# Two attention stages on one core: another order of VectorE's work inside each turn

## The reference, cut to what matters

```python
# sliding window, first block
scores = jnp.where(valid, scores + bias, NEG_INF)
probs = jax.nn.softmax(jnp.concatenate([scores, sink], axis=-1), axis=-1)[..., :-1]
out = jnp.einsum('bnhgqk,bnkhd->bnqhgd', probs, vb)
...
# chunk band and causal, second block
p = jax.nn.softmax(sc, axis=-1)
return jnp.einsum('bhqk,bhkd->bhqd', p, v)
```

## Time and profile before

| what | us |
|---|---|
| median of 3 executions | 1940.71 |
| lowest of them | 1938.64 |
| the profiled execution, its own time | 1938.64 |
| its span in the trace | 1936.6 |
| TensorE matmuls busy | 1904.5 (98% of the span) |
| TensorE weight loads busy | 1577.2 (81%) |
| VectorE busy | 968.0 (50%) |
| ScalarE busy | 778.3 (40%) |
| GpSimd busy | 92.8 (5%) |

### The profile page before, as it was taken

The page is one execution under the profiler, slowest core; times in us unless marked ns, Lnnn a source line. Parts: engine busy times, 40 slices in busy tenths (PEclk is TensorE's granted clock), DMA queues, the critical chain, the costliest instruction groups (busy, mean ns, idle before and its releaser), DMA issues.

```text
span 1936.6 us, 23640 instructions
## 1 busy us (share of the span) xinstructions
PE 1904.5 (98%) x9297; PEld 1577.2 (81%) x9297; DVE 968.0 (50%) x2069; ACT 778.3 (40%) x1482; POOL 92.8 (5%) x165
## 2 busy tenths in 40 slices
PE   8999999999999999999999999999999999999998
PEld 6888888868888888887888888888888888888887
DVE  5788764546676666665321244433343433333234
ACT  5566333347777777776211132312030312212022
POOL 4111001100000000000000000000000000000000
PEclk9999999999999999999999999999999999999999
DMA  5410124322232212222321141212020211112002
GB/s 169 115 34 28 55 87 152 102 67 66 61 77 72 74 52 64 74 61 59 95 54 44 55 159 48 66 44 66 22 76 23 75 33 55 55 33 66 22 22 87
DMA packets 132479, 129.29 MB, mean 67 GB/s; under 512 B 7233, under 2 KB 112265, under 8 KB 132370
## 3 DMA queue, kind: packets, MB, share of 16 engines
q1 hardware_dynamic: 126482, 115.18, 19.7%
q0 software_dynamic: 5888, 12.62, 2.9%
HBM read 105.70 MB, written 15.79 MB: 63 GB/s over the span
## 4 chain that ended last, share of the span: by engine, by line
PE 89%; DVE 6%; ACT 3%; issue 2%; DMA 0%; POOL 0%; DVEq 0%; POOLq 0%; SPq 0%; ACTq 0%
PE b L86 85%; PE b L89 4%; DVE Wf L108 1%; DVE Wr L97 1%; ACT Wf L94 1%; DVE Xr L97 1%; ACT Wf L93 1%; DVE Wf L97 1%; ACT Wr L93 1%; DVE ring L97 1%; ACT Xr L93 0%; DVE Yf L105 0%; DVE Wf L101 0%; DVE Yr L105 0%; ACT ring L93 0%
## 5 line engine op out<-in xcount | busy, mean ns | idle before, releaser
L86 PE MATMUL b<-Yr,ring 128*128 128x512 f32 x1920 | 507.9, 400 | 1.1 <-DVE Xr L97 1.1
L86 PE MATMUL b<-Xr,ring 128*128 128x512 f32 x1872 | 452.7, 393 | 3.3 <-DVE Xr L97 1.5
L86 PEld LDWEIGHTS b<-Xr,ring 128*128 128x128 f32 x1872 | 345.6, 189 | 70.9 <-issue 4.2
L86 PEld LDWEIGHTS b<-Yr,ring 128*128 128x128 f32 x1920 | 340.1, 189 | 56.0 <-DVE Xr L97 1.5
L86 PE MATMUL b<-Xr,Yr 128*128 128x512 f32 x1104 | 254.0, 390 | 0.0
L86 PEld LDWEIGHTS b<-Xr,Yr 128*128 128x128 f32 x1104 | 206.8, 188 | 42.8
L86 PE MATMUL b<-Yr 128*128 128x512 f32 (+2 forms) x1040 | 236.1, 375 | 0.0
L86 PEld LDWEIGHTS b<-Yr 128*128 128x128 f32 x1040 | 190.7, 188 | 38.1
L97 DVE TENSOR_TENSOR Wf<-Wf,b 128x512 f32<-128x512 f32 x144 | 92.6, 684 | 237.7 <-PE b L86 237.7
L93 ACT ACTIVATE Wf<-b 128x512 f32<-128x512 f32 (+3 forms) x215 | 106.2, 494 | 229.1 <-PE b L86 225.5
L94 ACT ACTIVATE Wf<-Wf,st 128x640 f32<-128x640 f32 (+3 forms) x192 | 125.2, 652 | 162.1 <-DVE st L112 58.8
(11 more groups left out here) (123 smaller groups left out, 1612.6 us busy)
## 6 DMA issues: line engine op xcount, KB each, us to landing
stage<-in_w_in_dram SPq DMA_DIRECT2D x58, 512.0 KB, 4.0
stage<-in_w_up_dram SPq DMA_DIRECT2D x32, 512.0 KB, 4.0
stage<-in_w_down_dram SPq DMA_DIRECT2D x32, 512.0 KB, 3.5
stage<-in_w_out_dram SPq DMA_DIRECT2D x16, 512.0 KB, 3.5
Xr<-Xr POOLq DMA_DIRECT2D x32, 256.0 KB, 3.4
Yf<-in_x_dram SPq DMA_DIRECT2D x8, 512.0 KB, 6.4
Wf<-in_x_dram SPq DMA_DIRECT2D x8, 512.0 KB, 4.4
scratch_x<-Wf SPq DMA_DIRECT2D x8, 512.0 KB, 2.7
```

What stands on the lines that cost most here:

```text
L86: return self.send(lambda e: e.matmul(o, w, a, start=start, stop=stop))
```

## The change

Only the order of VectorE's program inside a turn is changed, in both loops; no instruction is added or taken out, and the other engines' programs stay as they are.

- In both loops `p_low` moves from the head of the turn to behind top and shift. In swa it stands right behind the sink shift, in att behind `att_out`.
- In swa `one_over` and the normalising come before `swa_out` and `swa_ended`, no longer after them; in att `one_over` comes before `att_ended`.
- `swa_split` and `att_split` run one turn later: turn t takes the weights of turn t-2.

```diff
@@ swa @@
     for t, turn in enumerate(swa):
-        for step, g in turn.applied:
-            p_low("swa", step, g, m.pt1)
         if turn.slot is not None:
...
-        for step, g in (swa[t - 1].applied if t > 0 else ()):
-            if step.n % 2:
-                swa_out(dve, m, at, note, step.n)
-        if t:
-            swa_ended(t - 1, (0, 1, 2))
+        for step, g in turn.applied:
+            p_low("swa", step, g, m.pt1)
         if turn.slot is not None:
             one_over("swa", s, 7)
...
             sent.then_inc(m.v_sm, ("normed", "swa", s.n))
+        for step, g in (swa[t - 1].applied if t > 0 else ()):
+            if step.n % 2:
+                swa_out(dve, m, at, note, step.n)
         if t:
-            swa_split(t - 1)
+            swa_ended(t - 1, (0, 1, 2))
+        if t > 1:
+            swa_split(t - 2)
@@ att @@
     for t, turn in enumerate(att):
-        for step, g in turn.applied:
-            p_low("att", step, g, m.pt2)
         if turn.slot is not None:
...
                 att_out(dve, m, at, step)
-        if t:
-            att_ended(t - 1, (0, 1, 2))
+        for step, g in turn.applied:
+            p_low("att", step, g, m.pt2)
         if turn.slot is not None:
             one_over("att", s, 3)
         if t:
-            att_split(t - 1)
+            att_ended(t - 1, (0, 1, 2))
+        if t > 1:
+            att_split(t - 2)
```

More of the change, by code:

```diff
@@ L1688, in vector_program @@
             sent.then_inc(m.v_sm, ("normed", "swa", s.n))
+        for step, g in (swa[t - 1].applied if t > 0 else ()):
+            if step.n % 2:
+                swa_out(dve, m, at, note, step.n)
         if t:
-            swa_split(t - 1)
+            swa_ended(t - 1, (0, 1, 2))
+        if t > 1:
+            swa_split(t - 2)
     swa_ended(len(swa) - 1, (0, 1, 2))
     swa_ended(len(swa), (0, 1, 2))
-    swa_split(len(swa) - 1)
-    swa_split(len(swa))
+    for t in (len(swa) - 2, len(swa) - 1, len(swa)):
+        swa_split(t)
     def pool_mean(n):
@@ L1918, in vector_program @@
         if t:
-            att_split(t - 1)
+            att_ended(t - 1, (0, 1, 2))
+        if t > 1:
+            att_split(t - 2)
     att_ended(len(att) - 1, (0, 1, 2))
+    att_split(len(att) - 2)
     att_split(len(att) - 1)
```

## The result

| what | before | after |
|---|---|---|
| median (us) | 1939.24 | 1989.59 |
| executions | 1938.64, 1939.24, 1940.71 | 1989.43 to 1990.62 |
| ratio, 95% interval | 1 | 1.026, 1.024 to 1.028 |
| profiled execution, its own time | 1938.64 | 1990.36 |
| its span | 1936.6 | 1988.3 |

The account below looks back on a forecast made before the run. TensorE's program was taken as the critical path, with 32 us idle. The terms were 30 - 7.5 - 2 = 20 us in att and 8 in swa, so 1938.6 + 28 = 1967 us; the range ran from 1942 to 1990.

Parts of the forecast that it names:

- the banks of the transposes: In att, bank waits were said to have 3.3 us or more to spare, so to cost nothing.
- What bounds the kernel: TensorE's program is the critical path; it idles 32 us in all, the most any order of VectorE's work can remove.
- `p_low` behind top: In att, products wait for the later `p_low`: 11 us banded, 15.5 in three causal pairs, 3.5 in the last, together 30.
- the quarter taken off: In att, 7.5 us off the 30, since a TensorE wait moves its next turn back and gives VectorE time.
- `one_over` before `att_ended`: In att, normalised weights come earlier and TensorE's small waits for them go: -2 us.
- swa, +8 forecast: Swa: 6 us for turns with `q_low`, 4 with `split_low`, 1.6 others, less 2 of present waits and 1.5 overlap.
- Splits one turn later: Both loops: least distance from low part to matmul is 14 us in swa, 18 in att; cost nothing, loads likewise.
- The clock "stays 1.00": In the profile after, TensorE's granted clock was to stay 1.00.
- What a measurement can tell: Whole kernel: a difference of 2% (39 us) is about what a measurement can tell from none.
- A: Rival: waits are absorbed, lost tenths in one turn won back in the next; 1938 to 1946 us, chance 0.20.
- B: Rival: faster, all listed TensorE waits vanish (-10 us) and `p_low` is always ready; 1928 to 1937 us, chance 0.08.
- C: Rival: slower by over 2%; VectorE bounds swa, `att_ended` and splits ahead of top reach att's products whole; 1992 us, chance 0.16.

Follow-up runs that it names:

- e1: Kernel before with only `p_low` moved behind top and shift (in att behind `att_out`): 1981.58 us, ratio 1.0214.
- e6: Kernel after with `p_low` back at the head of the turn only for the first two groups of steps of four groups: 1984.59 us, ratio 1.0234.
- e3: Kernel before with only `one_over` and the normalising ahead of `swa_out`, `swa_ended` and `att_ended`: 1977.89 us, ratio 1.0195.
- e4: Kernel after with `att_split(t - 1)` and `swa_split(t - 1)` as before, so without later splits: 1998.95 us, ratio 1.0302.
- e8: Kernel after with the splits a turn earlier from turn 112 on, the last pair of att: 1981.46 us, ratio 1.0217.
- e2: Kernel before with only the splits one turn later, in both loops: 1949.78 us, ratio 1.0050.
- e11: Kernel before with `att_out` ahead of top in banded pairs except the first turn of eight, else between top and shift: 1933.57 us, ratio 0.9969.
- e5: Kernel after with `p_low` back at the head of the turn, all other parts kept: 1978.08 us, ratio 1.0198.
- e9: Kernel before with `att_out` between top and shift, and in swa `swa_out` behind the normalising: 1944.88 us, ratio 1.0028.
- e10: Kernel before with `p_low` behind top but ahead of shift: 1970.29 us, ratio 1.0161.
- e7: Kernel before with `att_out` ahead of top everywhere, `p_low` staying first: 1945.01 us, ratio 1.0027.

## Why the prediction was wrong, step by step

The forecast was 28 us more, 20 in att and 8 in swa; by the distances it is 41.7 in att (10.9, 19.2 and 11.6) and 10.5 in swa. Swa and the waits at the products came out near the sum. The steps that failed are three prices of the sum: the banks of the transposes, put at nothing (11 us measured); the later splits, put at nothing (9.4 us in the last pair, through the loads); and `one_over` ahead of `att_ended`, put at a gain of 2 us (it costs 23 us in att alone, 9.9 when `p_low` is late already).

*What bounds the kernel: not contradicted.* No order of VectorE's work that was run gained more than 7 us (the bound was 32), and every us lost shows as TensorE starting a matmul later.

*`p_low` behind top: the waits of single turns right, the list of waits too short.* Forecast were 30 us less a quarter, 22.5, all at products. By the distances e1's products lose 21.0 us over before at the matmuls that wait for `p_low` (8.9 in the banded pairs, 10.9 in the causal ones, 1.2 in the last) and 5.6 in the matmuls right behind them: 26.6, between 22.5 and 30. So the term was right to 4 us; the quarter taken off was too much. The step that failed is "bank waits in att have 3.3 us or more to spare: nothing". I took that spare time from `p_low` at the head and did not ask it again for `p_low` behind top: the causal transposes lose 9.0 us (e1 and after), the last pair 2.3. Of the causal 9.0 only 4.0 come back when the bank is free in time (e6), since the products behind them wait for the late `p_low` too. Whether a fourth bank would do more was not tried. In e1 1.4 us more are lost at the first transposes of att, which run at half clock (below).

*`one_over` before `att_ended`: wrong sign.* "These go: -2 us" counted what the normalised weights gain and only named what waits behind `att_ended`: "the next turn's top, `p_low` and so the products". Priced alone it is +23 us in att (e3: 12.3 and 10.8). The rows had it: the 68.0 us ahead of `one_over` are what is left when `att_ended` already fills part of that time; in e3 it is 104.9. Behind a late `p_low` the loss is smaller, 9.9 us (e4 against e1), since `p_low` fills part of the hole. In after the idle time ahead of `one_over` fell to 43.6 us (430 to 950; forecast: under 40):

```profile
L115 DVE RECIPROCAL st<-st 128x1 f32<-128x1 f32 x126 | 20.2, 160 | 43.6 <-ACT Wf L94 41.7
```

*swa, +8 forecast, 10.5 measured: right in kind.* From the end of the exponentials of turn 14 to the products of turn 15 it was 126.57 - 122.49 = 4.1 us; after, it is 132.78 - 127.68 = 5.1: 1.0 more, and about 1.1 was forecast for such a turn:

```profile
127.49 0.19 ACT L93 ACTIVATE st<-st 128x2 f32<-128x2 f32 x1
...
132.78 0.54 PEld L86 LDWEIGHTS b<-Wr 128*128 128x128 f32 x4 [0.53 <-DVE Wr L97]
```

By the distances 4.8 us are lost at products that wait for `p_low`, 2.6 at the bank that `q_low` frees, and 1.7 at a single wait that ends at 77.89. The parts that I took off against one another there hide larger ones: e3 alone loses 15.9 us in swa.

*Splits one turn later: "cost nothing" failed at one place, and in the rest the sign is the other.* I measured the distance from a low part to the matmul on it (14 us and more) and wrote that the loads "have the same slack". The load's slack is another: it starts when the split has freed `stage`, and ScalarE waits for it ahead of an exponential. That costs 9.4 us in the last pair (e8 against after) and 7.4 by itself (e2). In the loop the later split saves 17 us where the other parts are in (e4). The part forecast at zero is thus the one with the largest effect in both directions.

*The clock "stays 1.00": wrong,* by some 1 to 3 us at each of two places (below).

*What a measurement can tell: too coarse.* The prediction put it at 2% (39 us). The intervals here are 0.2% or less to either side, so 1967 us would have been told from before with ease, and e11's 0.3% is.

*The rivals.* A and B fell: in e1 only 3 to 4 of the 30 us at the products come back, and the kernel is slower. C gave the right total, and it was the one that read "`att_ended` and splits ahead of top reach the products whole". But its price was made of other terms (no quarter off, 0.3 us in 60 turns), and of splits it has the effect wrong, since they had been moved out of the turn of `att_ended`. So its total is luck in part: `att_ended` ahead of top is borne out (e3, e4), the splits are not, and the transposes (e1, e6) and the loads (e8) are in none of its terms.

What stays open: the parts' effects overlap (93 us alone, 50 together), and the runs give each part alone and two of the three pairs (e4, e5), not `p_low` with the later splits; how much of the causal 19.2 us belongs to which part can't be said from them. Whether more `stage` buffers would make the later split free was not tried.

## What to carry to other kernels

In an engine that works strictly in order, an instruction placed behind a wait is priced by the hole it leaves as much as by its own delay: ask for every wait of that engine what fills it now and what will stand in it after. Then test each part both alone and by taking it out of the whole: here the later split cost 10.9 us alone and saved 9.4 on top of the other two. When an instruction moves, list every resource that it releases (the product's operand, the PSUM bank, the staging buffer that a load waits for) and take the spare time of each again for the new place, and at the end of the loop as well as in its middle. Small work that is ready early belongs where the engine would idle, before the wait and not behind it; that was worth 0.3% here with the rest untouched (e11).

## What was unexpected of the hardware

Behind some waits TensorE's granted clock fell to half (1.2 of 2.4 GHz) for 3 to 10 us. Stretches of after: length, busy PE, PEld, DVE, ACT, POOL, clock, DMA.

```profile
911.00:917.50 6.50, 3.39 (x20) 2.58 (x20) 1.59 (x7) 2.40 (x6) 0.00 (x0) 0.96 0.35 91
917.50:921.00 3.50, 0.00 (x0) 0.00 (x0) 3.46 (x7) 1.82 (x4) 0.00 (x0) 0.50 0.36 107
921.00:928.00 7.00, 6.93 (x25) 5.71 (x26) 3.64 (x10) 3.07 (x8) 0.00 (x0) 0.56 0.60 180
77.50:81.00 3.50, 3.11 (x9) 2.56 (x10) 0.24 (x1) 0.00 (x0) 0.33 (x1) 0.54 0.00 0
```

The first three rows are the wait of 6.48 us (914.6 to 921.1) and what follows: the clock is at 0.50 in the wait's second half and 0.56 over the 7 us of work behind it. The last row stands around the end of a wait of 2.31 us. At half clock matmuls of 512 columns start every 0.43 us instead of every 0.23. The work done at half clock is about 6 us in the first case and 3 in the second, so some 3 and 1.4 us are lost: a wait can cost more than its length. Not each wait does it. The first transposes of att wait 2.62 us for ScalarE in before, with the clock at 1.00 from there on, and in e1, where it was 0.68. Before first, then e1:

```profile
428.00:432.00 4.00, 1.38 (x12) 1.20 (x12) 2.16 (x7) 2.89 (x7) 1.17 (x2) 1.00 0.35 71
```

```profile
436.00:440.00 4.00, 2.12 (x9) 2.10 (x10) 1.52 (x7) 2.20 (x7) 1.16 (x2) 0.68 0.59 130
```

The length of the wait does not tell the two apart. At this place seven of the thirteen traces show half clock and six do not: of those with a wait of 2.6 us e1, e9, e10 and e11 do and before, e2 and e7 do not, and of those with one of 2.1 us e3, e4 and e6 do and after, e5 and e8 do not. Nor is it the kernel alone: of the six executions of e11 two have a mean granted clock of 0.996 and took 1935.3 and 1935.6 us, the other four 0.997 to 0.999 and 1933.0 to 1933.8. What decides it isn't settled by these runs.
